# Scattering the router's gates with two rounded products: gates split in a high and a low part, the low one-hot matrices made by GpSimd

## What is computed

```python
eidx = jnp.take_along_axis(cidx, pos, axis=-1)            # (T, heads, 16), key0 * 128 + key1
gate = jax.nn.softmax(top_s.astype(jnp.float32), axis=-1)
u = jnp.take(expert_u, eidx, axis=0)
act = jax.nn.gelu(jnp.einsum('thkd,td->thk', u, xb))
v = jnp.take(expert_v, eidx, axis=0)
return jnp.einsum('thk,thkd->td', gate * act, v)
```

## Time and profile before

| | |
|---|---|
| median of 3 runs | 2393.5 us (2392.57 to 2398.09) |
| the profiled execution's own time | 2388.96 us |
| its span in the profile | 2387.6 us |
| PE busy over the span | 2278.5 us (95%) |
| DVE busy | 1777.1 us (74%) |
| ACT busy | 1095.6 us (46%) |
| POOL busy | 574.4 us (24%) |
| chain that ended last, by engine | PE 82%, DVE 7%, ACT 4%, issue 3%, DMA 3%, POOL 1% |

### The profile page before, as it was taken

One profiled execution on the slowest core, in us unless ns is written; L12 is line 12 of the kernel. 1 busy time (PEld: TensorE's weight loads), 2 busy tenths in 40 slices (PEclk: granted clock), 3 DMA queues, 4 the chain that ended last, 5 costly groups with the idle time before them and its releaser, 6 DMA issues.

```text
span 2387.6 us, 34419 instructions
## 1 busy us (share of the span) xinstructions
PE 2278.5 (95%) x12827; PEld 2012.0 (84%) x12827; DVE 1777.1 (74%) x3434; ACT 1095.6 (46%) x1956; POOL 574.4 (24%) x419
## 2 busy tenths in 40 slices
PE   7989999999999999999999998999888899999998
PEld 5768999999999999999999997688655577777766
DVE  7889869988899976888888886633577645477764
ACT  4232343333488863333333335422366623566662
POOL 4110357888722212222222211200000020000001
PEclk9999999999999999999999999999999999999998
DMA  6546558899989999999999992111100022100012
GB/s 259 186 159 221 194 181 287 310 311 316 324 278 335 330 330 335 345 355 362 335 341 352 352 335 92 53 62 62 36 1 1 18 62 84 40 23 23 23 36 71
DMA packets 162374, 466.79 MB, mean 196 GB/s; under 512 B 15520, under 2 KB 72992, under 8 KB 159776
## 3 DMA queue, kind: packets, MB, share of 16 engines
q1 hardware_dynamic: 100512, 305.19, 36.0%
q0 software_dynamic: 36864, 134.23, 16.1%
q10 hardware_dynamic: 24832, 25.17, 3.3%
HBM read 412.10 MB, written 52.43 MB: 195 GB/s over the span
## 4 chain that ended last, share of the span: by engine, by line
PE 82%; DVE 7%; ACT 4%; issue 3%; DMA 3%; POOL 1%; SPq 0%; ACTq 0%; DVEq 0%; POOLq 0%
PE psum L491 7%; PE psum L629 7%; PE psum L492 7%; PE psum L493 7%; PE psum L631 7%; PE psum L630 7%; PE psum L482 6%; PE psum L483 6%; PE psum L484 6%; PE psum L602 4%; PE psum L509 2%; PE psum L978 2%; PE psum L795 2%; DMA arena<-hidden 2%; DVE weights_low L1536 1%
## 5 line engine op out<-in xcount | busy, mean ns | idle before, releaser
L1027 ACT ACTIVATE weights_high<-arena 128x1024 fp32r<-128x1024 f32 x355 | 374.6, 1056 | 462.5 <-PE psum L631 324.0
L1536 DVE TENSOR_TENSOR weights_low<-arena,weights_high 128x1024 fp32r<-128x1024 f32 x266 | 331.7, 1247 | 225.8 <-ACT weights_high L1027 224.6
L629 PE MATMUL psum<-hidden_high,weights_high 128*128 128x384 f32 x1024 | 344.0, 336 | 6.4 <-issue 3.7
L491 PE MATMUL psum<-x_high,weights_high 128*128 128x384 f32 x1024 | 345.8, 338 | 4.1 <-POOL weights_low L2186 2.7
L630 PE MATMUL psum<-hidden_low,weights_high 128*128 128x384 f32 x1024 | 342.7, 335 | 0.0
L631 PE MATMUL psum<-hidden_high,weights_low 128*128 128x384 f32 x1024 | 342.6, 335 | 0.0
L492 PE MATMUL psum<-x_low,weights_high 128*128 128x384 f32 x1024 | 342.2, 334 | 0.0
L493 PE MATMUL psum<-x_high,weights_low 128*128 128x384 f32 x1024 | 342.2, 334 | 0.0
L482 PE MATMUL psum<-x_high,weights_high 128*128 128x512 f32 x696 | 276.8, 398 | 14.0 <-DVE weights_low L1536 9.1
L484 PE MATMUL psum<-x_high,weights_low 128*128 128x512 f32 x696 | 272.4, 391 | 0.0
L483 PE MATMUL psum<-x_low,weights_high 128*128 128x512 f32 x696 | 272.4, 391 | 0.0
(11 more groups left out here) (263 smaller groups left out, 4294.4 us busy)
## 6 DMA issues: line engine op xcount, KB each, us to landing
arena<-in_stream SPq DMA_DIRECT2D x227, 512.0 KB, 4.6
arena<-in_v_rows SPq DMA_DIRECT2D x128, 512.0 KB, 6.4
arena<-in_ada_w SPq DMA_DIRECT2D x48, 512.0 KB, 3.5
hidden<-arena SPq DMA_DIRECT2D x128, 192.0 KB, 4.5
router<-arena SPq DMA_DIRECT2D x12, 2048.0 KB, 9.3
arena<-hidden SPq DMA_DIRECT2D x128, 192.0 KB, 6.8
arena<-router ACTq DMA_DIRECT2D x16, 1536.0 KB, 20.2
arena<-in_pair_w SPq DMA_DIRECT2D x8, 640.0 KB, 3.9
```

The costliest lines, as they stand in the source:

```text
L491: PE.matmul(bank[b][:, 0:N], wh[w][:, k, :], xh[:, k, PICKED:T], start=k == 0, stop=False)
L629: PE.matmul(out, wh[w][:, n, :], hh[:, r, :], start=e == 0, stop=False)
L1027: ACT.activation(wh[BUFFER[u]], slots[u % RING], AF.Copy).then_inc(*tick("weights_high", u))
L1536: DVE.tensor_tensor(wl[BUFFER[u]], slots[u % RING], wh[BUFFER[u]].bitcast(F32), ALU.subtract).then_inc(*tick("weights", u))
```

## The change

The f32 product of the scatter is replaced by two products of rounded numbers with the same stationary matrix hot1, which is exact when rounded (zeros and ones). The gate is split: gate_high is the gate rounded by ACT (one more ACTIVATE behind the copies of `entry`), and DVE subtracts it from `entry[2]`, which from then on holds the low part. DVE makes hot0 from gate_high, as many instructions as before. POOL makes hot0_low, four TENSOR_SCALAR per quad in four buffers, in front of the fetches of the same unit, and waits before each quad until quad i - 4 is scattered. PE waits for hot0_low too.

```diff
-    hot1 = area(43, 16, KEYS)
-    hot0 = area(76, 16, KEYS)
+    hot1, hot0 = rounded("hot1", 43, 16, KEYS), rounded("hot0_high", 76, 16, KEYS)
+    hot0_low = [rounded(f"hot0_low{i}", first, QUAD, KEYS) for i, first in enumerate((82, 83, 47, 88))]
+    gate_high = rounded("gate_high", 85, T)
@@ scatter, on PE
             PE.wait_ge(*at("hot0", i))
+            PE.wait_ge(*at("hot0_low", i))
...
             for j in range(QUAD):
-                last = PE.matmul(bank[b][:, j * KEYS:(j + 1) * KEYS], hot1[:, b * QUAD + j, :],
-                                 hot0[:, b * QUAD + j, :], start=True, stop=True)
+                out, place = bank[b][:, j * KEYS:(j + 1) * KEYS], hot1[:, b * QUAD + j, :]
+                PE.matmul(out, place, hot0[:, b * QUAD + j, :], start=True, stop=False)
+                last = PE.matmul(out, place, hot0_low[b][:, j, :], start=False, stop=True)
@@ one_hots, on ACT
-            ACT.activation(group, group, AF.Relu, bias=ones[:, 0:1], scale=-1.0).then_inc(*tick("hot1_odd", i))
+            ACT.activation(group, group.bitcast(F32), AF.Relu, bias=ones[:, 0:1], scale=-1.0).then_inc(*tick("hot1_odd", i))
@@ ahead of the scatter, on ACT
+        ACT.activation(gate_high[:, PICKED:T], bank[2][:, PICKED:T], AF.Copy).then_inc(*tick("entered", "high"))
@@ one_hots, on DVE
-                last = DVE.tensor_scalar(hot0[:, b * QUAD + j, :], iota, entry[0][:, t:t + 1], entry[2][:, t:t + 1],
-                                         ALU.is_equal, ALU.mult)
+                last = DVE.tensor_scalar(hot0[:, b * QUAD + j, :], iota, entry[0][:, t:t + 1],
+                                         gate_high[:, t:t + 1].bitcast(F32), ALU.is_equal, ALU.mult)
@@ ahead of them, on DVE
-        DVE.wait_ge(*at("entered", 2))
+        DVE.wait_ge(*at("entered", "high"))
+        DVE.tensor_tensor(entry[2][:, PICKED:T], entry[2][:, PICKED:T], gate_high[:, PICKED:T].bitcast(F32),
+                          ALU.subtract).then_inc(*tick("gate_low", 0))
@@ on GpSimd
+        def hot0_lows(i):
+            if i >= 4:
+                POOL.wait_ge(*at("scattered", i - 4))
+            for j in range(QUAD):
+                t = PICKED + i * QUAD + j
+                last = POOL.tensor_scalar(hot0_low[i % 4][:, j, :], iota, entry[0][:, t:t + 1], entry[2][:, t:t + 1],
+                                          ALU.is_equal, ALU.mult)
+            last.then_inc(*tick("hot0_low", i))
+
+        POOL.wait_ge(*at("gate_low", 0))
         for kind, n in ROW_STEPS[JOBS:]:
+            if kind == "up":
+                for i in range(quads_before(n - 1), quads_before(n)):
+                    hot0_lows(i)
             for j in ROWS_AT[kind, n]:
                 fetch_row(j + ROW_RING)
```

## The result

| | before | after |
|---|---|---|
| median of the runs made side by side | 2393.03 us (4 runs, 2388.88 to 2398.09) | 2605.82 us (4 runs, 2601.17 to 2611.85) |
| span of the profiled execution | 2387.6 us | 2604.8 us |
| PE / DVE / ACT / POOL busy | 2278.5 / 1777.1 / 1095.6 / 574.4 us | 2369.1 / 1799.6 / 1100.5 / 943.6 us |

The ratio is 1.0888, with a 95% interval of 1.0869 to 1.0908: the change costs 213 us where 77 were forecast, and 2606 lies above the range. The sign was right, the size was not.

A forecast was written before the change was run, and what follows sets the result against it. PE and DVE were both full in the scatter; POOL's turns would raise DVE from 6.65 to 9.17 us a unit. From 2389, adding 75 and 2 gave 2466, plus 4.5 for the median: 2470 us, range 2412 to 2570.

The forecast's parts named there:

- The bound before, and the ceiling: Scatter: PE paces at 6.84 us a unit, DVE needs 6.65; infinitely fast PE would gain 6 us, 0.25%.
- PE: Scatter products: 24 rounded ones a unit at 0.11 us each, 2.6 us (1.4 to 3.9); no gain sure.
- DVE and the rounded type: DVE's one-hots in the scatter: as many as before, and the rounded type costs nothing.
- A turn's price for DVE: Scatter: each of POOL's twelve instructions a unit takes 0.21 us from DVE (0.10 to 0.48), making its unit 9.17 us.
- POOL's own time: POOL in the scatter: fetches 1.4 us plus twelve turns of about 0.26 + 0.21, 5.6 us; 7.1 a unit.
- Rival D: GpSimd bounds the scatter: its TENSOR_SCALAR takes 0.8 us or more, 11.5 a unit, 2544 us and above; chance 0.09.
- The stretch itself: POOL in the scatter: two or three turns beside large DVE instructions add some 0.9 us each, 9.4 a unit.
- B: Scatter: only DVE's two-input instructions contend with POOL, at most 3.8 turns a unit, 7.45 us, 2416 in all; chance 0.12.
- C: Scatter: POOL's instructions take nothing from DVE, so the kernel isn't slower, 2389.5 or 2395 us; chance 0.10.
- E: PE's pauses in the scatter lower its clock, costing some 2 us a unit more, near 2530 us; chance 0.03.
- The added waits: POOL's waits in the scatter: fetches have three units of lead, `use_row` won't notice; POOL and DVE pace each other.
- The start: Ahead of the scatter loop: a fourth ACT copy, the subtraction and POOL's first four lows add 2 us, once.

The follow-up runs named there:

- 9: Changed kernel, but POOL's TENSOR_SCALAR for the low one-hots only compares, with one pointer; 2525.16 us, ratio 1.0563 to before.
- experiment 10: Changed kernel, but POOL's TENSOR_SCALAR adds and multiplies by constants, without comparison or pointers; 2434.74 us, ratio 1.0187 to before.
- experiment 2: Changed kernel, but DVE instead of POOL makes the low one-hots; 2484.95 us, ratio 1.0401 to before.
- experiment 3: Changed kernel without POOL's low one-hots: both rounded products read the high one-hot; 2394.52 us, ratio 1.0010 to before.
- experiment 4: Changed kernel without POOL's low one-hots and with one rounded product alone, on the high one-hot; 2385.37 us, ratio 0.9986 to before.
- experiments 5: Changed kernel with the low one-hots shared: two of each quad's four on POOL, two on DVE; 2473.96 us, ratio 1.0351 to before.
- 6: Changed kernel with one low one-hot a quad on POOL, read by all four products; 2407.36 us, ratio 1.0067 to before.
- Experiment 1: Kernel before, with batches of small instructions appended behind its end, on POOL with DVE idle, then on both; 2523 us, 134 more than before.

## Why the prediction was wrong, step by step

In the table, POOL's low is the mean length of its record, and POOL's sum is twelve of them and the fetches.

| kernel | POOL, one low (us) | POOL's sum a unit | DVE's work a unit | unit | granted clock |
|---|---|---|---|---|---|
| changed | 0.94 | 13.1 | 7.21 | 13.26 | 0.75 |
| 9, comparison only | 0.75 | 10.7 | 7.25 | 10.78 | 0.82 |
| 10, constants | 0.40 | 6.4 | 8.08 | 8.28 | 0.91 |
| 2, lows on DVE | none | 1.5 | 9.69 | 9.69 | 0.86 |
| 3, products only | none | 1.6 | 6.6 | 6.80 | 1.00 |

**The bound before, and the ceiling.** Right. DVE's 6.65 us came out as 6.64 in experiment 4, where nothing else was in its way, and no version could have gained more than the few us that it gained.

**PE.** Right. 0.11 us for a rounded product of 128 columns with its load, chosen between 0.06 and 0.16, is what experiment 3 shows, and two cost what one f32 product did.

**DVE and the rounded type.** Right. Twice the TENSOR_SCALAR in experiment 2 kept their pace of 0.256.

**A turn's price for DVE.** Right in kind, too high in size. The forecast took 0.21 us, bounds 0.10 to 0.48. With DVE full or nearly so it was 0.10 to 0.15 (experiments 5, 6, 10), and in the changed kernel, where 167 of POOL's 384 instructions have no DVE instruction beside them, 0.047. By this term with the correct size the sum would have been 6.65 + 12 x 0.12 = 8.1 us a unit and some 2436 us, which is what experiment 10 measured. By the Trainium skill (SBUF — State Buffer, section "Who interferes with whom") the loser waits for the whole instruction of the other. The runs agree for two inputs on POOL (0.80 and 0.96 us) and disagree for one: 0.05 to 0.15 us is lost beside an instruction of 0.78.

**POOL's own time. This is the step that failed.** "Twelve turns of about 0.26 + 0.21" allowed POOL's instruction 0.47 us, the wait for a DVE instruction included, and the argument against rival D was that "a two-input instruction of twice the width needs 0.81". The instruction takes 0.777 us alone and 0.93 in the loop. The bound was taken across kinds: a two-input subtraction was supposed to be dearer than any one-input instruction. Experiment 1 shows that a subtraction of the same 128 columns takes 0.412, a comparison with one pointer scalar 0.580, and the one used 0.777. The memset was no lower bound of use either. Worked out with what was measured, POOL's unit is 12 x 0.777 = 9.3, the stretch beside DVE 12 x 0.15 = 1.8, the fetches 1.8, idle 0.3: 13.26 us before rounding, and 32 x (13.26 - 6.84) = 205 us where the forecast had 75. These 130 us are nearly the whole miss of 136. The prediction's own sum for POOL, 9.4 us a unit, becomes 13.1 with 9.3 in place of its 5.6.

The stretch itself was foreseen and not far off: the prediction added 1.8 to 2.7 us a unit to POOL's side for "two or three turns beside large ones". In the changed kernel 120 of POOL's 384 instructions have a two-input DVE instruction beside them; these last 1.24 us in the mean and carry 54 of the 58 us of stretch, and the other 264 last 0.80. One of the 120, beside a two-input instruction of DVE (L1743) that starts at 794.46 and takes 1.21:

```profile
794.28 1.98 POOL L2206 TENSOR_SCALAR hot_low<-con,arena 128x128 fp32r<-128x128 f32 x1
```

The Trainium skill (GPSIMD Engine Reference, "Elementwise — side-by-side cycle accounting") has 1.03 cycles per element where the read and write port is the limit, from which the prediction made an estimate of 0.11 us for 128 columns. The runs disagree for this instruction: 0.777 us is seven times that, and even its share by the column, 3.3 ns, is four times 1.03 cycles at 1.2 GHz.

**Rival D** named this mechanism, its condition (0.8 us or more), and 11.5 us a unit "or more"; it got 0.09. Its sign, POOL busy without a gap, is what the profile shows. It was still 1.8 us a unit short, which is the stretch beside DVE (12 x 0.15 = 1.8) that it left out. No row of before held a comparison on POOL, and 38 us for 0.1 us of a turn was named as what the forecast fails by: POOL's own time deserved the same sentence, since it entered 12 times a unit too.

**The other rivals.** B and C spoke of DVE alone and are passed by. E's condition came true, its price didn't show: the granted clock was 0.75 in the stage with PE waiting 107.8 us for POOL, but in 2, 9 and 10 it was 0.82 to 0.91 and the unit was DVE's or POOL's sum all the same. The changed kernel's own share of it wasn't separated; POOL is idle for some 10 us of the stage's 421, and no more than that can be the slower PE's.

**The added waits.** Right that fetches have lead enough; `use_row` doesn't appear among the waits. Right also that POOL and DVE could pace each other. Experiment 5 is that case, with both nearly full.

**The start.** Forecast 2 us, measured 5, and another 6 between the last scatter product and the first down product, which had not been foreseen: PE stands 9.55 us ahead of its first down product, where it stood 3.67, and the profile names no engine that it waits for. Neither was tested on its own.

## What to carry to other kernels

Before work is moved to GpSimd, time one instruction of exactly that form there (operation, pointers or constants, width): among one-input instructions of one width the price differed by a factor of three, and it was the whole outcome here. Then make the sum for both engines, GpSimd's with the other one busy: here GpSimd's instructions stretched beside VectorE's two-input work, and where GpSimd's own instruction had two inputs, VectorE lost 0.8 us to each as well. And where the engine that one wants to relieve stands only 0.19 us a unit above the next one (6.84 and 6.65 here), first take the product away altogether, as experiment 4 did: it shows the most that any such change can bring.

## What the runs showed of the hardware

- A TENSOR_SCALAR of 128x128 on GpSimd takes 0.263 us with an addition, a multiplication and constants, 0.607 with a comparison in place of the addition, 0.58 with a comparison or a multiplication alone by one pointer scalar, 0.777 with both by two; the last costs 3.3 ns a column from 128 to 512. Why a comparison or a pointer costs so much stays open.
- Who loses depends on the inputs. One-input GpSimd instructions are held by VectorE's two-input ones (starts 3.85, 3.50, 2.44 us apart instead of 0.78) and hardly by its TENSOR_SCALAR (0.825), and cost it 0.05 to 0.15 us each. GpSimd's two-input ones of 512 columns take turns one for one with VectorE's TENSOR_SCALAR (1.22 us apart instead of 0.256). Why GpSimd is held for two or three instructions and not for one isn't known.
- Two rounded products of 128 columns, each with its load of 128, take as long as one f32 product, 0.22 us (experiment 3); the rounded type is free for VectorE (0.256 us in experiment 2, as before) and for GpSimd (0.777 with it and without).
- The granted clock of TensorE followed its waiting: 1.00 with PE full (3), 0.91, 0.86, 0.82 and 0.75 as the unit grew from 8.3 to 13.3 us, with no price of its own to be seen in the units of 2, 9 and 10.
